# The order of rounding and eviction on ScalarE in the u products of a PEER layer

## The chip, the cores and the metric

The kernel runs on one core of a Trainium2 chip. A core has five engines that run their own instruction streams and meet only at semaphores: TensorE (PE in the profile, with its weight loads as PEld), VectorE (DVE), ScalarE (ACT), GpSimd (POOL) and SyncE (SP), which here only issues DMAs. The metric is the device time of one execution in microseconds. Before the change the median of three runs is 1938.89 us, between 1938.2 and 1939.08.

## What is computed

The reference is one residual block on 512 tokens of width 1024: a token mixer (mLSTM and differential attention), then a PEER layer. The change lies in the PEER layer, whose heart is

```
scores = einsum("thcd,hcnd->thcn", qry, sub_keys)          # 8 heads x 2 halves x 128 keys
s_top, i_top = top_k(scores, 16)                           # per half
best_s, best_pos = top_k(s_top0[:, None] + s_top1[None], 16)  # 16 of 128*128 experts
gates = softmax(best_s)
act = gelu(einsum("td,thkd->thk", h, expert_u[idx]))
out = einsum("thk,thkd->td", act * gates, expert_v[idx])
```

The kernel does this densely for 384 of the tokens' gates and 320 of their activations: it multiplies all 16384 experts in 128 tiles of 128 experts (the u products), takes Gelu of everything, multiplies by a matrix of gates that is zero almost everywhere, and multiplies by expert_v (the v products). The other tokens' experts are gathered row by row and computed on VectorE beside the products.

## The kernel before, in words

All products are float32 made of three fp32r products. An operand is cut into a rounded part (hi) and a rest (lo), and hi x hi, hi x lo and lo x hi are added.

In the stage of the u products (`experts_block`, line 2089) one step n is one tile of 128 experts:

- SP (`every`, L2176) loads raw tile n into a ring of 4 buffers, once tile n-4 has been cut (`lo_done`). Behind it SP stores the activations of tile n-4 to DRAM, after their eviction (`gelu_done`). The last 24 tiles are kept in SBUF and have no store. In some steps SP writes a piece of the gate matrix (`flush`, L2193), four pieces in four steps that follow each other, twice in each group of 16 steps.
- ScalarE rounds the raw tile: `cut` (L2351), in_uhi<-con_raw at L2356. It waits for the tile to land and for product n-2 to end, since uhi has two buffers.
- VectorE subtracts: `cut` (L2463), in_ulo<-con_raw,in_uhi at L2466.
- TensorE runs the product of tile n: 24 matmuls of 128x320 (L2274), after `lo_done` of n and the eviction of n-2 (`gelu_done`), since the sums ps_u have two buffers.
- ScalarE evicts the sums of tile n with Gelu (L2393, for the kept tiles L2395) after `u_done`.

In the first 60 steps VectorE also does the routing of the four blocks of 128 tokens (`route`, ten pieces, one a step). One piece needs an exponential on ScalarE (L2383). In the next 48 steps, the gate steps, there are one-hot matrices for the gates: VectorE makes them (L2640, L2641), ScalarE scales the rows of one (`gated_rows`, L2404, eight instructions), TensorE multiplies them after the product (16 matmuls, L2302), and ScalarE evicts the two banks (`gates`, L2415). The last 20 steps are plain. In about seven of nine gate steps, and in some of the others, VectorE works on gathered rows, and for some of these ScalarE weighs one column (L1997, L1999). Each engine runs its list in the written order. Nothing reorders it.

In ScalarE's list before the change, step n (`every`, L2367) is: the rounding of tile n+1, the small items, the wait for product n, and the eviction of tile n; then in a gate step the two evictions of gates. L2425 is a single Gelu whose result SP waits for (L2211) in one step.

Of the kernel before, what the change touches and what calls it, by code (L numbers as in the profile page):

```python
# [53 lines left out]
def wait(eng, sem, value):  # L54

    if isinstance(value, int) and value <= 0:
        return
    eng.wait_ge(sem, value)
# [1696 lines left out]
NEXP = NK  # L1755
# [333 lines left out]
def experts_block(nc, con, ring, hot, hot_all, stage, early, got, rt, A, hT, acts, gmat, x1, dst, vhi, vlo, cut_hi, cut_lo):  # L2089
# [3 lines left out]
    with Alloc(nc, "xin") as al:  # L2093
# [255 lines left out]
        @block.scalar  # L2349
        def _(act):  # L2350
            def cut(n):  # L2351

                act.wait_ge(landed[n % U_RING], 16 * (n // U_RING + 1))

                wait(act, u_done, n - 1)
                act.activation(uhi[n % 2][:], cut_of[n % U_RING], ACT.Copy).then_inc(hi_done, 1)  # L2356

            def rounded(n):
                s = n % RING
                act.wait_ge(v_in[s], 16 * (n // RING + 1))  # L2360

                wait(act, used, n - RING + 1)
                act.activation(vhi[s][:], v[s], ACT.Copy).then_inc(vhi_done, 1)  # L2363
                act.wait_ge(wt_done, n + 1)
                act.activation(whi[s][:].rearrange("p (b t) -> p b t", t=8 * G_TOK), weights(n), ACT.Copy).then_inc(whi_done, 1)

            def every(n):  # L2367
                if n < NEXP - 1:

                    cut(n + 1)  # L2370
                if n == 2:
                    act.activation(opts, con.iota[:, 0:TOPK].unsqueeze(2).to_broadcast([P, TOPK, SLOTS]),
                                   ACT.Copy).then_inc(tables, 1)
                if n > 0:
                    for r in IN_AT[n - 1]:
                        got.weigh(act, r)
                if n == NEXP - 1:
                    for h in range(2):
                        act.wait_ge(flushed[h], 64 * (N_HOT // G_STEPS))
                    rounded(0)  # L2380
                if n in EXP_AT:
                    act.wait_ge(sub_done, EXP_AT[n] + 1)
                    act.activation(ge, eg, ACT.Exp).then_inc(exp_done, 1)  # L2383
                if N_HOT0 - 1 <= n < N_TAIL0 - 1:
                    gated_rows(n + 1 - N_HOT0)
                act.wait_ge(u_done, n + 1)

                if n < STORED + RING:
                    wait(act, kept[n % 4], 16 * (n // 4))
                elif n == NEXP - in_room:  # L2390
                    act.wait_ge(flushed[0], 64 * (N_HOT // G_STEPS))
                if n < STORED:
                    act.activation(act_t[n % 4][:], ps_u[n % 2][:, 0:TU], ACT.Gelu).then_inc(gelu_done, 1)  # L2393
                else:
                    act.activation(held[n - STORED], by_block(ps_u[n % 2][:, 0:TU]), ACT.Gelu).then_inc(gelu_done, 1)  # L2395

            def gated_rows(m):

                if m == N_HOT - SIDE // G_TOK:
                    act.wait_ge(late_done, 1)  # L2400
                act.wait_ge(is_row, m + 1)
                for i in range(G_TOK):
                    at = m * G_TOK + i
                    op = act.activation(hot_i[m % 2][:, i, :], hot_i[m % 2][:, i, :], ACT.Copy, scale=slot[2][:, at:at + 1])  # L2404
                op.then_inc(gated, 1)

            def gates(gi, q):
                m = G_STEPS * gi + q
                for b in range(2):
                    act.wait_ge(g_done, 2 * m + b + 1)  # L2410
                    if q % 8 == 0 and b == 0:

                        wait(act, flushed[q // 8], 64 * gi)
                    t0 = (q % 8) * G_TOK + 4 * b
                    act.activation(stage[q // 8][:, :, t0:t0 + 4], ps_g[b].rearrange("p t i -> p i t"),  # L2415
                                   ACT.Copy).then_inc(staged, 1)

            for n in range(NEXP):
                every(n)
                if N_HOT0 <= n < N_HOT0 + N_HOT:  # L2420
                    gates((n - N_HOT0) // G_STEPS, (n - N_HOT0) % G_STEPS)
                if n == SIDE_LAST + 2:
                    last = SIDE_ENTRIES[-1]
                    act.wait_ge(got.row_free[last % ROWS], last // ROWS + 1)
                    act.activation(got.side_dots[:], got.side_dots[:], ACT.Gelu).then_inc(got.side_raw_done, 1)  # L2425
            for n in range(NEXP):
                if n > 0:
                    rounded(n)
                for r in OUT_AT[n - 1] if n else IN_AT[NEXP - 1]:
                    got.weigh(act, r)  # L2430
                if n == END:
                    act.wait_ge(got.row_free[MAIN[-1] % ROWS], MAIN[-1] // ROWS + 1)
                    act.activation(junk, got.acc[:], ACT.Square, accum_out=ss0[:]).then_inc(ss0_done, 1)
            wait(act, ss0_done, 1)
            for m in range(2 * ND):
                act.wait_ge(closed, m + 1)

                wait(act, ss_done, m)
                act.activation(junk[:, 0:512], out[m // 2][m % 2][:], ACT.Square,
                               accum_out=ss[:, m:m + 1]).then_inc(ss_done, 1)  # L2440
# [367 lines left out]
```

## Time and profile before

| | |
|---|---|
| median of 3 runs | 1938.89 us |
| profiled execution, its own time | 1935.99 us |
| its span in the profile | 1934.3 us |
| TensorE busy (PE) | 1863.7 us, 96% |
| VectorE busy | 1485.3 us, 77% |
| ScalarE busy | 819.3 us, 42% |
| stage of the u products | about 823 to 1378 us |
| stage of the v products | about 1378 to 1934 us |
| granted TensorE clock, mean | 0.992 of full speed |

The span runs from the first to the last instruction; the execution's own time is 1.7 us longer. Matmuls overlap, so a duration of 0.31 us stands beside a pitch of 0.147 us, and only the idle time of TensorE says what it lost. "Idle before, releaser" says how long an engine stood still ahead of an instruction and what ended that. An idle time of an engine that is not the bottleneck costs nothing.

### The profile page before, as it was taken

The page shows a single profiled execution, that of the slowest core. Times are in us where ns is not written, and L with a number is a line of the kernel's source. Part 1 is how long each engine was busy: PE and PEld are TensorE (multiplying, and loading weights), DVE is VectorE, ACT ScalarE, POOL GpSimd, SP SyncE. Part 2 cuts the span into 40 slices and gives each one's busy share as a digit, 9 for nine tenths or more (in the row PEclk, how much of TensorE's full clock was granted, in tenths as well). Part 3 has the DMA queues.
Part 4 walks back from the last instruction along what each step waited for, and adds up shares of the span by engine and source line. Part 5 has one row for each costly group of instructions (what it writes and reads, how often), then busy time and mean ns, then how long its engine had stood idle before and what let it go on. Part 6 is the DMA issues. An engine that isn't in the chain of part 4 may idle for free.

```text
span 1934.3 us, 28426 instructions
## 1 busy us (share of the span) xinstructions
PE 1863.7 (96%) x10366; PEld 1628.5 (84%) x10366; DVE 1485.3 (77%) x2847; ACT 819.3 (42%) x1719; POOL 550.6 (28%) x295
## 2 busy tenths in 40 slices
PE   7999999999999989999999999999999999899997
PEld 4788777888877888899999999999888778788776
DVE  4777545355466645789999999996899889899986
ACT  4110233110253253344445989884444444444443
POOL 0343201344211213201224553231244233333320
PEclk9999999999999999999999999999999999999999
DMA  7335410354211514166878899999999999999993
GB/s 284 88 109 174 152 44 23 130 199 149 75 56 44 175 52 129 66 183 225 322 273 288 304 378 362 391 391 394 346 405 414 408 412 412 390 411 412 411 391 132
DMA packets 194876, 483.68 MB, mean 250 GB/s; under 512 B 16216, under 2 KB 126992, under 8 KB 175568
## 3 DMA queue, kind: packets, MB, share of 16 engines
q1 hardware_dynamic: 166416, 314.50, 45.2%
q0 software_dynamic: 27648, 167.78, 22.0%
q8 instruction: 57, 0.93, 0.2%
q14 instruction: 51, 0.42, 0.1%
q10 hardware_dynamic: 704, 0.04, 0.0%
HBM read 435.55 MB, written 46.40 MB: 249 GB/s over the span
## 4 chain that ended last, share of the span: by engine, by line
PE 21%; DVE 20%; DMA 12%; issue 3%; ACT 1%; SPq 0%; DVEq 0%; POOLq 0%; POOL 0%; ACTq 0%
PE xin_ps_u L2274 15%; DMA experts_hot<-act_scratch 5%; DMA con_raw<-in_expert_v 4%; DVE experts_acc L2015 4%; DVE experts_rows L1988 4%; PE xin_out L2302 3%; DVE over_v_vlo L2655 3%; DMA con_raw<-in_expert_u 3%; PE xin_out L2327 2%; DVE xin_wlo L2658 2%; DVE in_ulo L2466 2%; DVE experts_rows L1977 1%; DVE xin_g L2652 1%; DVE experts_hot L2652 1%; ACT in_uhi L2356 1%
## 5 line engine op out<-in xcount | busy, mean ns | idle before, releaser
L1970 POOL DMA_INDIRECT experts_rows<-in_expert_rows,experts_idx x128 | 232.1, 1813 | 490.4 <-DVE experts_acc L2015 460.8
L2274 PE MATMUL xin_ps_u<-con_h_hi,in_uhi 128*128 128x320 f32 x1024 | 322.7, 315 | 9.7 <-DVE in_ulo L2466 6.7
L2274 PE MATMUL xin_ps_u<-con_h_lo,in_uhi 128*128 128x320 f32 x1024 | 317.1, 310 | 0.0
L2274 PE MATMUL xin_ps_u<-con_h_hi,in_ulo 128*128 128x320 f32 x1024 | 317.0, 310 | 0.0
L2327 PE MATMUL xin_out<-over_v_vhi,xin_whi 128*128 128x512 f32 x768 | 242.2, 394 | 15.3 <-DVE xin_wlo L2658 15.2
L2327 PE MATMUL xin_out<-over_v_vlo,xin_whi 128*128 128x512 f32 x768 | 239.7, 391 | 0.0
L2327 PE MATMUL xin_out<-over_v_vhi,xin_wlo 128*128 128x512 f32 x768 | 239.3, 390 | 0.0
L2274 PEld LDWEIGHTS xin_ps_u<-con_h_hi,in_uhi 128*128 128x128 f32 x1024 | 192.9, 188 | 14.4 <-DVE in_ulo L2466 11.1
L540 POOL TENSOR_TENSOR weights_wlo<-con_raw,weights_whi 128x2048 fp32r<-128x2048 f32 x29 | 133.7, 4611 | 221.7 <-DVE weights_whi L624 215.6
L2274 PEld LDWEIGHTS xin_ps_u<-con_h_lo,in_uhi 128*128 128x128 f32 x1024 | 193.1, 189 | 0.0
L2274 PEld LDWEIGHTS xin_ps_u<-con_h_hi,in_ulo 128*128 128x128 f32 x1024 | 192.8, 188 | 0.0
L2466 DVE TENSOR_TENSOR in_ulo<-con_raw,in_uhi 128x1024 fp32r<-128x1024 f32 x127 | 155.9, 1228 | 46.5 <-ACT in_uhi L2356 46.1
L2327 PEld LDWEIGHTS xin_out<-over_v_vhi,xin_whi 128*128 128x128 f32 x768 | 142.5, 189 | 54.9 <-DVE over_v_vlo L2655 19.1
L1965 POOL DMA_INDIRECT experts_rows<-in_expert_rows,experts_side_at x64 | 103.2, 1612 | 249.1 <-DVE experts_rows L1977 132.6
L2327 PEld LDWEIGHTS xin_out<-over_v_vhi,xin_wlo 128*128 128x128 f32 x768 | 144.7, 188 | 30.6
L2327 PEld LDWEIGHTS xin_out<-over_v_vlo,xin_whi 128*128 128x128 f32 x768 | 144.7, 188 | 30.5
L2363 ACT ACTIVATE over_v_vhi<-con_raw 128x1024 fp32r<-128x1024 f32 x128 | 134.6, 1051 | 75.2 <-DMA con_raw<-in_expert_v 73.3
L2015 DVE SCALAR_TENSOR_TENSOR experts_acc<-experts_rows,experts_coef,experts_acc 128x1024 f32<-128x1024 f32 x127 | 162.1, 1277 | 0.6 <-ACT experts_coef L1999 0.6
L2655 DVE TENSOR_TENSOR over_v_vlo<-con_raw,over_v_vhi 128x1024 fp32r<-128x1024 f32 x128 | 155.7, 1217 | 3.3 <-ACT over_v_vhi L2363 3.3
L1988 DVE SCALAR_TENSOR_TENSOR experts_rows<-experts_rows,con_h 128x1024 f32<-128x1024 f32 x128 | 155.7, 1216 | 0.0
L2356 ACT ACTIVATE in_uhi<-con_raw 128x1024 fp32r<-128x1024 f32 x127 | 133.6, 1052 | 9.1 <-DMA con_raw<-in_expert_u 8.8
L2404 ACT ACTIVATE experts_hot<-experts_hot,in_slot 128x128 f32<-128x128 f32 x384 | 117.3, 390 | 10.8 <-DVE experts_hot L2640 10.0
(478 smaller groups left out, 3859.3 us busy)
## 6 DMA issues: line engine op xcount, KB each, us to landing
con_raw<-in_expert_u SPq DMA_DIRECT2D x128, 512.0 KB, 7.0
con_raw<-in_expert_v SPq DMA_DIRECT2D x128, 512.0 KB, 11.3
con_raw<-in_w_in SPq DMA_DIRECT2D x36, 1024.0 KB, 6.0
act_scratch<-in_act SPq DMA_DIRECT2D x104, 160.0 KB, 4.3
experts_hot<-act_scratch SPq DMA_DIRECT2D x104, 160.0 KB, 12.4
gate_scratch<-in_stage SPq DMA_DIRECT2D x12, 1024.0 KB, 11.2
gate_scratch<-over_s_stage SPq DMA_DIRECT2D x12, 1024.0 KB, 12.4
experts_hot<-gate_scratch SPq DMA_DIRECT2D x16, 768.0 KB, 13.4
```

The source lines that it names most:

```text
L540: pool.tensor_tensor(wlo[s][:], raw[s][:], as_f32(whi[s][:]), ALU.subtract).then_inc(w_lo, 1)
L1965: pool.indirect_dma_start(out=self.rows[:, s, half * D:(half + 1) * D], out_offset=None, in_=halves, in_offset=bass.IndirectOffsetOnAxis(a ...
L1970: pool.indirect_dma_start(out=self.rows[:, s, :], out_offset=None, in_=rows, in_offset=bass.IndirectOffsetOnAxis(ap=self.idx[:, r:r + 1], ...
L1988: dve.scalar_tensor_tensor(out=u, in0=u, scalar=1.0, in1=con.h0[:], op0=ALU.mult, op1=ALU.mult, accum_out=self.coef[:, r:r + 1]).then_inc( ...
L2015: dve.scalar_tensor_tensor(out=self.acc[:], in0=v, scalar=self.coef[:, r:r + 1], in1=self.acc[:], op0=ALU.mult, op1=ALU.add).then_inc(self ...
L2274: mm = pe.matmul(ps_u[s % 2][:, 0:TU], a[s % 2][:, k, :], m[:, k, P:P + TU], start=(i == 0), stop=(i == 3 * KD - 1))
L2327: product = lambda s, t, h, w, m, **flags: pe.matmul(out[t][h][:], w[s][:, t * P:(t + 1) * P], m[s][:, h * 512:(h + 1) * 512], **flags)
L2356: act.activation(uhi[n % 2][:], cut_of[n % U_RING], ACT.Copy).then_inc(hi_done, 1)
L2363: act.activation(vhi[s][:], v[s], ACT.Copy).then_inc(vhi_done, 1)
L2404: op = act.activation(hot_i[m % 2][:, i, :], hot_i[m % 2][:, i, :], ACT.Copy, scale=slot[2][:, at:at + 1])
L2466: dve.tensor_tensor(ulo[n % 2][:], cut_of[n % U_RING], as_f32(uhi[n % 2][:]), ALU.subtract).then_inc(lo_done, 1)
L2655: dve.tensor_tensor(vlo[s][:], v[s], as_f32(vhi[s][:]), ALU.subtract).then_inc(vlo_done, 1)
```

## The change

On ScalarE the rounding of tile n+2 now stands in step n, between the wait for product n and the eviction of tile n. The rounding of tile 1 stays ahead of everything. Every tile is still rounded once, and the waits of each instruction are on the same semaphores and values.

```diff
             def every(n):
-                if n < NEXP - 1:
-
-                    cut(n + 1)
+                if n == 0:
+                    cut(1)
                 if n == 2:
                     act.activation(opts, con.iota[:, 0:TOPK].unsqueeze(2).to_broadcast([P, TOPK, SLOTS]),
                                    ACT.Copy).then_inc(tables, 1)
...
                 if N_HOT0 - 1 <= n < N_TAIL0 - 1:
                     gated_rows(n + 1 - N_HOT0)
                 act.wait_ge(u_done, n + 1)
+                if n < NEXP - 2:
+
+                    cut(n + 2)
 
                 if n < STORED + RING:
                     wait(act, kept[n % 4], 16 * (n // 4))
```

The lines below L2371 move down by two: the evictions are L2395 and L2397 after the change, the subtraction L2468, and the evictions of gates L2417.

ScalarE in a step with the exponential, of the kernel before (L2356 rounds, L2393 evicts a product, L2383 is the exponential):

```order
L2356 ACTIVATE in_uhi<-con_raw 128x1024
L2383 ACT_TABLE_LOAD
L2383 ACTIVATE over_s_stage<-over_s_stage 128x128
L2393 ACT_TABLE_LOAD
L2393 ACTIVATE in_act<-xin_ps_u 128x320
L2356 ACTIVATE in_uhi<-con_raw 128x1024
```

The same place of the changed kernel (L2395 evicts, L2382 is the exponential):

```order
L2395 ACTIVATE in_act<-xin_ps_u 128x320
L2382 ACT_TABLE_LOAD
L2382 ACTIVATE over_s_stage<-over_s_stage 128x128
L2356 ACTIVATE in_uhi<-con_raw 128x1024
L2395 ACT_TABLE_LOAD
L2395 ACTIVATE in_act<-xin_ps_u 128x320
```

The rounding that followed Gelu's table load and the eviction now stands ahead of both.

ScalarE in a gate step with a gathered row, of the kernel before (L2404 scales the one-hot rows, L2415 evicts the gate products):

```order
L2356 ACTIVATE in_uhi<-con_raw 128x1024
L1997 ACTIVATE experts_coef<-experts_coef 128x1
L1999 ACTIVATE experts_coef<-experts_coef,experts_gate 128x1
L2404 ACTIVATE experts_hot<-experts_hot,in_slot 128x128 x8
L2393 ACTIVATE in_act<-xin_ps_u 128x320
L2415 ACTIVATE in_stage<-xin_out 128x128x4 x2
```

And of the changed kernel (the same lines, L2406, L2395 and L2417 there):

```order
L1997 ACTIVATE experts_coef<-experts_coef 128x1
L1999 ACTIVATE experts_coef<-experts_coef,experts_gate 128x1
L2406 ACTIVATE experts_hot<-experts_hot,in_slot 128x128 x8
L2356 ACTIVATE in_uhi<-con_raw 128x1024
L2395 ACTIVATE in_act<-xin_ps_u 128x320
L2417 ACTIVATE in_stage<-xin_out 128x128x4 x2
```

The rounding moved ahead of three evictions, that of the product and the two of the gates. The lists of the other engines are the same.

## Rows read from the trace of the kernel before

**Rows 1.** Busy time of each engine in four stretches: us, engines, PEclk, DMA share, GB/s.

```profile
820.00:1046.00 226.00, 217.87 (x1469) 214.18 (x1467) 204.53 (x644) 101.41 (x145) 45.57 (x32) 1.00 0.74 248
1046.00:1306.00 260.00, 257.11 (x1919) 256.19 (x1920) 250.41 (x278) 232.24 (x607) 99.66 (x55) 0.99 0.98 365
1306.00:1378.00 72.00, 71.75 (x489) 71.34 (x488) 48.96 (x53) 33.00 (x63) 11.43 (x11) 1.00 0.98 366
1378.00:1934.00 556.00, 532.20 (x2302) 431.18 (x2300) 501.74 (x702) 235.85 (x468) 180.99 (x100) 0.99 0.96 382
```

**Rows 2.** Groups by line, 820 to 1378: busy us, mean ns | idle before, releasers.

```profile
L2274 PEld LDWEIGHTS xin_ps_u<-con_h_hi,in_uhi 128*128 128x128 f32 x1024 | 192.9, 188 | 14.4 <-DVE in_ulo L2466 11.1 <-issue 3.2
L2466 DVE TENSOR_TENSOR in_ulo<-con_raw,in_uhi 128x1024 fp32r<-128x1024 f32 x127 | 155.9, 1228 | 46.5 <-ACT in_uhi L2356 46.1
L2356 ACT ACTIVATE in_uhi<-con_raw 128x1024 fp32r<-128x1024 f32 x127 | 133.6, 1052 | 9.1 <-DMA con_raw<-in_expert_u 8.8 <-PEq L97 0.3
```

**Rows 3.** ScalarE in order of time: start, us, instruction, idle before and releaser.

```profile
902.77 0.44 ACT L2393 ACTIVATE in_act<-xin_ps_u 128x320 f32<-128x320 f32 x1 [2.46 <-PE xin_ps_u L2274]
...
906.29 0.44 ACT L2393 ACTIVATE in_act<-xin_ps_u 128x320 f32<-128x320 f32 x1 [2.14 <-PE xin_ps_u L2274]
...
909.32 1.28 ACT L2393 ACT_TABLE_LOAD   x1
910.61 0.44 ACT L2393 ACTIVATE in_act<-xin_ps_u 128x320 f32<-128x320 f32 x1
910.95 1.05 ACT L2356 ACTIVATE in_uhi<-con_raw 128x1024 fp32r<-128x1024 f32 x1
```

**Rows 4.** VectorE in order of time, at three places of the routing.

```profile
867.12 1.23 DVE L2466 TENSOR_TENSOR in_ulo<-con_raw,in_uhi 128x1024 fp32r<-128x1024 f32 x1 [0.73 <-ACT in_uhi L2356]
...
911.11 0.29 DVE L2527 TENSOR_TENSOR experts_gate<-over_s_stage,in_ginv 128x128 f32<-128x128 f32 x1
912.03 1.23 DVE L2466 TENSOR_TENSOR in_ulo<-con_raw,in_uhi 128x1024 fp32r<-128x1024 f32 x1 [0.62 <-ACT in_uhi L2356]
...
975.80 1.23 DVE L2466 TENSOR_TENSOR in_ulo<-con_raw,in_uhi 128x1024 fp32r<-128x1024 f32 x1 [0.20 <-ACT in_uhi L2356]
```

**Rows 5.** First weight loads of u products that had waited, three of eighteen.

```profile
918.21 0.19 PEld L2274 LDWEIGHTS xin_ps_u<-con_h_hi,in_uhi 128*128 128x128 f32 x1 [1.39 <-DVE in_ulo L2466]
...
1221.10 0.19 PEld L2274 LDWEIGHTS xin_ps_u<-con_h_hi,in_uhi 128*128 128x128 f32 x1 [1.07 <-DVE in_ulo L2466]
...
1345.45 0.19 PEld L2274 LDWEIGHTS xin_ps_u<-con_h_hi,in_uhi 128*128 128x128 f32 x1 [0.52 <-DVE in_ulo L2466]
```

**Rows 6.** SP's waits, 820 to 1380: us in total, times, longest.

```profile
SPq L2184 <- ACT in_act L2393: 298.5, 94, 6.1
...
SPq L2211 <- ACT experts_side_dots L2425: 6.8, 1, 6.8
```

**Rows 7.** Loads of u tiles: all 128 (KB, median us to landing), then one.

```profile
con_raw<-in_expert_u SPq DMA_DIRECT2D x128, 512.0 KB, 7.0
...
L2180 SPq DMA_DIRECT2D con_raw<-in_expert_u x1: 488/488/488, 914.2 to 914.2; - x1
...
DMA to landing us min/median/max: 10.7/10.7/10.7
```

**Rows 8.** ScalarE in order of time: one rounding, then two late tiles.

```profile
925.89 1.06 ACT L2356 ACTIVATE in_uhi<-con_raw 128x1024 fp32r<-128x1024 f32 x1
...
1208.30 1.06 ACT L2415 ACTIVATE over_s_stage<-xin_out 128x512 f32<-128x512 f32 x2
1211.93 1.06 ACT L2356 ACTIVATE in_uhi<-con_raw 128x1024 fp32r<-128x1024 f32 x1 [2.58 <-DMA con_raw<-in_expert_u]
...
1218.73 1.06 ACT L2356 ACTIVATE in_uhi<-con_raw 128x1024 fp32r<-128x1024 f32 x1 [1.70 <-DMA con_raw<-in_expert_u]
```

**Rows 9.** TensorE in order of time, at tile 60.

```profile
1046.26 0.39 PE L2274 MATMUL xin_ps_u<-con_h_hi,in_uhi 128*128 128x320 f32 x1 [1.87 <-issue]
...
1046.78 0.47 PE L2274 MATMUL xin_ps_u<-con_h_hi,in_uhi 128*128 128x320 f32 x1
```

## The prediction

> **What bounds the kernel now.** I read first how busy each engine is in each stretch of the stage [rows 1]. The u products run from 820 to 1378 us. TensorE is busy for 217.87 of 226 us in the first stretch (routing on VectorE), for 257.11 of 260 us in the second (the gate steps), for 71.75 of 72 us in the tail. So TensorE bounds the stage, and all its idle time there is 11.3 us. After it, in the v stage (1378 to 1934), the DMA share is 0.96 over the whole and TensorE has 24 us of idle time. The change leaves that stage alone, and what is won or lost before 1378 shifts it whole.
>
> Second, the groups by line [rows 2]. The first weight load of a u product sat idle for 14.4 us, of which 11.1 ended with in_ulo, the DVE subtraction (L2466). That subtraction waited 46.1 us for in_uhi, ScalarE's rounding (L2356), and the rounding 8.8 us for a DMA. So there is a chain: tile landed, rounding, subtraction, product. The change moves its second link.
>
> Third, the order in time on ScalarE, DVE and the weight loads [rows 3 to 5]. Plain evictions start as soon as the product ends; two of them, at 902.77 and 906.29, are 3.52 us apart: the pitch of a plain step. The rounding follows its eviction (910.61) at 910.95, so the eviction holds it back by 0.34 us. A gate step is 260/49 = 5.31 us [rows 1].
>
> Fourth, what the transfers wait for [rows 6 to 8]. SP issues the load of tile j+5 behind the store of tile j, and the store waits for the eviction of j: 298.5 us of waiting in 94 waits.
>
> **What the change does, part by part.** Nothing is added or removed: 127 roundings of 1052 ns stay [rows 2], as do the evictions. Tile n+2's rounding now starts when product n ends, and the eviction of n about 0.95 us later (a rounding takes 1.05 us, and the next instruction starts 0.1 us before its end, as 910.61 + 0.44 against 910.95 shows).
>
> 1. Plain steps, most of them: the rounding comes 0.34 us earlier, and neither TensorE nor DVE needs it: the product that wants it begins a full 3.52 us later, and the chain after the rounding is 1.05 + 1.23 us. Worth nothing. It counts only where DVE has fallen behind and goes on without a pause until TensorE waits. At 867.12 DVE waited 0.73 us for the rounding [rows 4]; all 0.34 us comes back. At 975.80 it waited 0.20 us, so 0.20 comes back. Sum: 0.54 us. If DVE had other work there it would be 0, the lower bound.
>
> 2. The steps with the exponential. ScalarE loads the exponential's table, then at 909.32 Gelu's, evicts at 910.61, and rounds at 910.95 [rows 3]. The product had ended at 906.29 + 3.52 = 909.81. In the new order the rounding starts there, ahead of the table load, 1.14 us earlier. DVE was done with its own work at 911.11 + 0.29 = 911.40 and began the subtraction at 912.03 [rows 4]. Its work began with a subtraction that itself comes 0.34 us earlier, so it is free at 911.06, and the rounding is done at 910.86. The subtraction starts at about 911.1, 0.93 us earlier. DVE then works without a pause to the product at 918.21, for which TensorE waited 1.39 us [rows 5]. So 0.93 us comes back. The pattern stands three times. From each I take 0.3 off, for loads (next step): 3 x 0.63 = 1.9 us. Bounds: 3 x 0 if DVE's own work fills in, 3 x 1.14 = 3.4.
>
> 3. The loads of this stretch. An eviction 0.95 us later lets the store and the next load start that much later, and the rounding wants its tile 0.34 us sooner. Load and rounding lose 1.3 us of margin. A load issued at 914.2 took 10.7 us [rows 7], so landed at 924.9; its tile was rounded at 925.89 [rows 8]: 1.0 us of margin, with gathered rows in flight beside it. So that rounding starts not 0.93 us earlier, but 0.6; that is the 0.3 above. The median load of the stage takes 7.0 us [rows 7], and from the eviction that releases it to the rounding that wants it there are three pitches, 10.6 us. With 3.6 us of margin it loses nothing.
>
> The evicted tile itself: product n needs the eviction of n-2. At 909.81 + 1.05 + 1.28 + 0.44 the eviction ends at 912.6, and the product that needs it starts at 913.0. It is hidden, with 0.4 us over.
>
> 4. The gate steps. Before: eviction, two evictions of the gate products (1.06 us for both [rows 8]), rounding. After: rounding, then the three. The rounding comes 0.34 + 1.06 us earlier, and more where ScalarE waited for the gate products. TensorE, busy for 257.11 of 260 us, hardly waits for it, so I count nothing. But the rounding waits for its DMA, and now the evictions stand behind that wait, where they stood ahead of it. At 1211.93 and 1218.73 ScalarE waited 2.58 and 1.70 us for tiles landing [rows 8]. TensorE's gate products need the gate evictions of the step before. Once a tile lands, 1.05 + 0.34 + 0.6 = 2.0 us go by until the first gate bank is free, and the pitch is 5.31 us. So TensorE stands still when a tile lands over 3.3 us after the product's end; before it did only at 4.8 us (5.31 us of pitch and a gate block of 5.31 - 3.52 = 1.8, less 1.05 of rounding and 1.23 of subtraction). The wait does not show in the trace of before. By these rows the tile of 1218.73 holds the gate products until 1218.73 + 2.0 = 1220.7 and the next product to about 1222.4, against 1221.10 [rows 5]: a loss of 1.3 us, the value taken. A second place like it, near 1260, where a tile landed just in time, costs 0.5 us by the same sum. Bounds: 0 (the later loads make up for it) and five bursts of gate flushes at 1.3 us each, 6.5.
>
> One more wait is in this place: SP stood 6.8 us for L2425 [rows 6], and in the new order L2425 comes 0.4 us later. That is within the 1.3.
>
> 5. The tail. Its tiles are kept in SBUF, no store stands ahead of the load, and the load waits for the subtraction alone. That is 0.34 us earlier, so loads start 0.3 us earlier and the wait of 0.52 us at 1345.45 [rows 5] shrinks by 0.3. Bounds 0 and 0.52.
>
> Sum: -0.54 - 1.9 + 1.3 + 0.5 - 0.3 = -0.9 us, to which I add nothing for the v stage. Against the profiled execution (1935.99 us, span 1934.3) this is 1935.1. The median of the runs is 1938.89, 2.9 us above that execution; on its scale the forecast is 1938.0.
>
> The rule that speaks against the change: in rows 7 and 8 one load had 1.0 us of margin and two had none. The Trainium skill's "DMA: Bandwidth & Descriptors", in its rules for kernel authors, says to issue a DMA early, compute, and wait on its semaphore late. The change does the reverse on both ends. What it would cost here is the third rival below, whose time comes from the rows.
>
> **The rivals.** What this kernel's measurement can tell from no change is about 0.2%, 3.9 us.
>
> Faster. The 2.4 us of steps 1 and 2 arrive, and step 4 costs nothing. On top, TensorE's pause of 1.87 us at 1046.26 is shortened: behind it the granted clock fell, and the matmuls took 0.47 instead of 0.31 us [rows 9]. That product took 5.29 instead of 3.51 us. If the clock stays up, 1.8 us come back. Sum: -2.4 - 0.3 - 1.8 = -4.5, so 1934.4. For it: the bound of step 2. Against: the pause is behind DVE's work without a gap, so it moves as a whole and keeps its length.
>
> Slower. The evictions behind a landing tile hold up the gate products and the next load in each of the five flush bursts, where the DMA share over the stretch is 0.98 [rows 1]. 5 x 1.3 = 6.5, and one pause of about 2 us drops the clock as at 1046, +1.8, less 2.7 won: +5.6, so 1944.5. It decides as soon as more than two tiles land 3.3 us late. For it: loads take 10 us and more there, and a late eviction starts a later load, which feeds itself. Against: between the bursts there are steps without flushes, in which the margins return, and the stretch of before lost under 3 us of TensorE in all.
>
> No effect. ScalarE's rounding was never what DVE lacked, since other work fills in: 1938.9. The waits of 0.62 and 0.73 us [rows 4] speak against it.
>
> **How the numbers follow.** The forecast 0.55, no effect 0.06, the faster rival 0.21, the slower one 0.18. The first two lie within 0.2%, so same 0.61, faster 0.21, slower 0.18. The forecast's own range, from the bounds of steps 1 to 5 that are near their rows, is 1935.5 to 1941. The range for 8 in 10 reaches to both rivals: 1933.5 to 1944.5.
>
> **What would show it.** Right: the wait at about 918 falls from 1.39 to under 0.7 us, likewise its two fellows; DVE's wait for in_uhi falls from 46.1 to near 30 us (0.34 us in each of 48 waits); the product of tile 60 starts about 2.4 us earlier than 1046.26; ScalarE's wait for landing tiles rises from 8.8 us; gate products (L2302) show a new wait for the evictions (L2417 after) near 1220. Wrong: TensorE's idle time from 820 to 1046 unchanged (step 2); no wait of L2302 on ScalarE (step 4); TensorE losing over 6 us from 1046 to 1306 (the slower rival); a start of the v stage that moved while the end did not, or the other way round.

## The result, and the profile after

The kernel became slower: median 1947.91 us against 1939.08 us of the kernel before, 15 runs each. The ratio is 1.0036, its 95% interval 1.0025 to 1.0048, so 4.8 to 9.3 us. The forecast was 1938.0 with a range up to 1944.5. One execution of 4785.03 us, among the six of the kernel with the early rounding in the gate steps alone (below), lies far outside all others and is left out of its ratio and median.

The profiled execution after is one of 1951.13 us, span 1949.4: 15.1 us longer than that of before, where the medians differ by 8.8. Busy time of each engine in four stretches, columns as in [rows 1]:

```profile
820.00:1046.00 226.00, 220.17 (x1488) 216.77 (x1486) 205.07 (x653) 101.04 (x139) 45.57 (x31) 1.00 0.72 245
1046.00:1306.00 260.00, 251.90 (x1867) 250.54 (x1866) 247.34 (x274) 225.01 (x597) 94.20 (x55) 0.99 0.96 353
1306.00:1378.00 72.00, 68.48 (x464) 68.25 (x463) 45.72 (x49) 33.24 (x69) 9.17 (x9) 0.98 0.97 372
1378.00:1934.00 556.00, 538.28 (x2353) 437.95 (x2352) 505.83 (x700) 239.60 (x472) 176.49 (x100) 0.99 0.97 385
```

Against [rows 1] TensorE has 2.3 us less idle time in the first stretch (1.0 when counted from the start of the stage, below) and 5.2 us more in the second (8.1 against 2.9), while the DMA share there fell from 0.98 to 0.96. The stretches no longer hold the same steps, so I went by the first and last instruction of each kind. The gate products of before, then of after (ns of one, then first and last start):

```profile
L2302 PE MATMUL xin_out<-experts_hot x768: 270/275/275, 1051.4 to 1306.2; 128*128 128x128 f32 x192
```

```profile
L2302 PE MATMUL xin_out<-experts_hot x768: 270/275/422, 1053.3 to 1317.9; 128*128 128x128 f32 x192
```

The gate stretch is 254.8 us before and 264.6 after. The same reading for all stages, in us (a few of the experiments below are in the table too; one profile each):

| kernel | u start | u start to tile 60 | gate stretch | v start | span |
|---|---|---|---|---|---|
| before | 823.1 | 223.1 | 254.8 | 1377.2 | 1934.3 |
| after | 826.0 | 222.2 | 264.6 | 1389.1 | 1949.4 |
| early in routing only | 823.1 | 221.5 | 255.2 | 1374.2 | 1934.3 |
| early in gate steps only | 824.6 | 223.2 | 261.8 | 1385.9 | 1945.6 |
| after, late store | 824.0 | 219.7 | 257.6 | 1376.9 | 1935.8 |
| gate steps, late store | 823.3 | 223.4 | 255.4 | 1377.8 | 1933.7 |

Of the 15.1 us, 2.9 lie ahead of the stage, where nothing changed, 9.0 in the u products (554.1 against 563.1), and 3.2 behind them; this is how much single executions differ outside the change. The 9.0 are +9.8 in the gate stretch and about -1 in the routing.

What waits for what, by lines (820 to 1395; columns as in [rows 2]):

```profile
L2274 PEld LDWEIGHTS xin_ps_u<-con_h_hi,in_uhi 128*128 128x128 f32 x1024 | 193.7, 189 | 11.1 <-DVE in_ulo L2468 7.3 <-issue 3.7
L2468 DVE TENSOR_TENSOR in_ulo<-con_raw,in_uhi 128x1024 fp32r<-128x1024 f32 x127 | 156.0, 1229 | 51.3 <-ACT in_uhi L2356 51.0
```

And as a list of waits over the same stretch (engine, who waited, for whom: us in total, times, longest):

```profile
ACT in_uhi L2356 <- DMA con_raw<-in_expert_u: 15.0, 7, 4.3
PEld xin_out L2302 <- issue: 9.3, 5, 3.8
PE xin_out L2302 <- ACT over_s_stage L2417: 5.3, 2, 3.5
PE xin_out L2302 <- ACT in_stage L2417: 2.7, 1, 2.7
```

```profile
SPq L2184 <- ACT in_act L2395: 295.7, 93, 8.7
```

The u product's wait for the subtraction fell from 11.1 to 7.3 us [rows 2]: the chain that the change shortens did get shorter. In its place the gate products (L2302) wait for ScalarE's eviction, and ScalarE for landing tiles, 15.0 us against 8.8. SP's longest wait for an eviction rose from 6.1 [rows 6] to 8.7.

The list has only part of ScalarE's waits for tiles: where ScalarE also waited for a product, it can put a wait for a landing down to PE or to "issue". I therefore matched each of the 48 tiles rounded in the gate stretch with the landing of its own load, in one profile of each kernel. "Late" is a rounding that starts within 0.1 us of the landing. The last column is how long after the end of a product its eviction starts.

| kernel | late tiles | ScalarE idle ahead of them, us | landing to rounding, median us | product's end to its eviction, median us |
|---|---|---|---|---|
| before | 5 | 7.8 | 5.9 | 0.9 |
| after | 14 | 23.8 | 3.6 | 2.0 |
| gate steps, late store | 6 | 10.4 | 6.1 | 1.7 |
| after, late store | 3 | 8.5 | 6.6 | 1.5 |

So the margin of a typical tile shrank by 2.3 us, and the tiles that had almost none before came late.

The first of these places, on the weight loads, ScalarE and SP of the kernel after (start, us, instruction, idle before):

```profile
1178.41 2.65 PEld L2302 LDWEIGHTS xin_out<-experts_hot 128*128 128x128 f32 x16 [2.96 <-issue]
1213.83 1.86 PEld L2302 LDWEIGHTS xin_out<-experts_hot 128*128 128x128 f32 x16 [2.02 <-issue]
1315.18 2.87 PEld L2302 LDWEIGHTS xin_out<-experts_hot 128*128 128x128 f32 x16 [3.75 <-issue]
```

```profile
1176.43 1.06 ACT L2356 ACTIVATE in_uhi<-con_raw 128x1024 fp32r<-128x1024 f32 x1 [4.88 <-PE xin_ps_u L2274]
1177.39 0.42 ACT L2395 ACTIVATE in_act<-xin_ps_u 128x320 f32<-128x320 f32 x1
1177.71 1.08 ACT L2417 ACTIVATE in_stage<-xin_out 128x512 f32<-128x512 f32 x2
```

```profile
1160.31 3.62 SPq L2180 DMA_DIRECT2D con_raw<-in_expert_u  x1
...
1166.85 0.45 SPq L2180 DMA_DIRECT2D con_raw<-in_expert_u  x1
...
1168.64 0.48 SPq L2180 DMA_DIRECT2D con_raw<-in_expert_u  x1
1177.84 0.32 SPq L2184 DMA_DIRECT2D act_scratch<-in_act  x1
1178.20 0.43 SPq L2180 DMA_DIRECT2D con_raw<-in_expert_u  x1
```

The load issued at 1160.31 took 16.0 us to landing:

```profile
L2180 SPq DMA_DIRECT2D con_raw<-in_expert_u x1: 3621/3621/3621, 1160.3 to 1160.3; - x1
...
DMA to landing us min/median/max: 16.0/16.0/16.0
```

Read these together. The tile landed at 1160.3 + 16.0 = 1176.3 and ScalarE rounded it at 1176.43, after 4.88 us of standing still. The row names PE as the releaser, but the product that this rounding waits for had long ended; it was the DMA, whose landing time fits to 0.1 us. Behind the rounding came the product's eviction (1177.39) and the gates' (1177.71), and with the first gate bank free the gate products went on at 1178.41. The product's eviction also let SP issue its store at 1177.84 and, behind it in SP's list, the next load at 1178.20, 9.6 us after the last one. The same stretch of the kernel before has loads every 3.3 to 5.7 us there:

```profile
1161.56 0.49 SPq L2180 DMA_DIRECT2D con_raw<-in_expert_u  x1
1164.51 0.32 SPq L2184 DMA_DIRECT2D act_scratch<-in_act  x1
1164.88 0.50 SPq L2180 DMA_DIRECT2D con_raw<-in_expert_u  x1
1170.21 0.32 SPq L2184 DMA_DIRECT2D act_scratch<-in_act  x1
1170.58 0.44 SPq L2180 DMA_DIRECT2D con_raw<-in_expert_u  x1
```

So a late tile delays the next load. That is a loop: landing, rounding, eviction, store, load, landing. From 1045 to 1320 us four pairs of neighbouring loads lie over 8 us apart (9.6, 12.5, 8.7 and 8.5); in the kernel before it is one (14.9). After a pause of TensorE the sixteen weight loads of the gates took 2.65 and 2.87 us instead of 1.86: the granted clock had fallen for a while. From here to 1232, then to 1318, and below them the same windows of the kernel before:

```profile
1172.00:1232.00 60.00, 53.91 (x390) 53.25 (x390) 51.61 (x57) 48.67 (x132) 13.68 (x8) 0.97 0.91 340
1232.00:1318.00 86.00, 82.46 (x617) 81.99 (x615) 78.09 (x80) 74.50 (x201) 18.88 (x12) 0.99 0.99 370
```

```profile
1172.00:1232.00 60.00, 57.55 (x434) 57.17 (x433) 55.76 (x60) 52.49 (x144) 15.89 (x8) 1.00 0.96 363
1232.00:1318.00 86.00, 85.96 (x640) 85.77 (x640) 79.52 (x82) 74.45 (x197) 24.81 (x14) 1.00 1.02 383
```

Here are 9.6 us of TensorE's idle time, where the kernel before has 2.5, and 0.03 x 60 + 0.01 x 86 = 2.7 us by the clock. In the first of the two the DMA share is 0.91 against 0.96: the DMA engines had room while tiles were late. This fits loads that were issued late. It does not show that as the only reason, since the landing of 16.0 us was itself long (the load of the same tile took 13.0 before).

### The profile page after: what moved, and what is told of

It reads as the page before. It is cut to its first block, busy times and chain, and to the rows that moved or that the text cites. A ratio compares the mean times of both kernels' runs of the same rounds, so it can differ in the third digit from the quotient of the medians.

```text
span 1949.4 us, 28321 instructions
## 1 busy us (share of the span) xinstructions
PE 1870.0 (96%) x10366; PEld 1633.4 (84%) x10366; DVE 1488.2 (76%) x2847; ACT 816.7 (42%) x1719; POOL 539.3 (28%) x295
## 4 chain that ended last, share of the span: by engine, by line
PE 21%; DVE 17%; DMA 14%; issue 2%; ACT 1%; SPq 1%; DVEq 0%; POOLq 0%; POOL 0%; ACTq 0%
PE xin_ps_u L2274 16%; DMA experts_hot<-act_scratch 7%; DMA con_raw<-in_expert_v 4%; DVE experts_rows L1988 3%; DVE experts_acc L2015 3%; PE xin_out L2302 3%; DVE over_v_vlo L2657 3%; DMA con_raw<-in_expert_u 3%; PE xin_out L2327 2%; DVE xin_wlo L2660 2%; DVE in_ulo L2468 1%; DVE experts_rows L1977 1%; DVE xin_g L2654 1%; DVE experts_hot L2654 1%; ACT in_uhi L2356 1%
## 5 line engine op out<-in xcount | busy, mean ns | idle before, releaser
L1970 POOL DMA_INDIRECT experts_rows<-in_expert_rows,experts_idx x128 | 219.3, 1714 | 516.6 <-DVE experts_acc L2015 482.6
L2356 ACT ACTIVATE in_uhi<-con_raw 128x1024 fp32r<-128x1024 f32 x127 | 134.2, 1057 | 180.5 <-PE xin_ps_u L2274 146.5
L2274 PEld LDWEIGHTS xin_ps_u<-con_h_hi,in_uhi 128*128 128x128 f32 x1024 | 193.7, 189 | 11.1 <-DVE in_ulo L2468 7.3
L540 POOL TENSOR_TENSOR weights_wlo<-con_raw,weights_whi 128x2048 fp32r<-128x2048 f32 x29 | 133.7, 4610 | 223.2 <-DVE weights_whi L624 217.1
L2468 DVE TENSOR_TENSOR in_ulo<-con_raw,in_uhi 128x1024 fp32r<-128x1024 f32 x127 | 156.0, 1229 | 51.3 <-ACT in_uhi L2356 51.0
L2406 ACT ACTIVATE experts_hot<-experts_hot,in_slot 128x128 f32<-128x128 f32 x384 | 117.5, 392 | 16.7 <-DVE experts_hot L2642 16.4
```

The costliest lines, as they stand in the source:

```text
L540: pool.tensor_tensor(wlo[s][:], raw[s][:], as_f32(whi[s][:]), ALU.subtract).then_inc(w_lo, 1)
L1970: pool.indirect_dma_start(out=self.rows[:, s, :], out_offset=None, in_=rows, in_offset=bass.IndirectOffsetOnAxis(ap=self.idx[:, r:r + 1], ...
L2274: mm = pe.matmul(ps_u[s % 2][:, 0:TU], a[s % 2][:, k, :], m[:, k, P:P + TU], start=(i == 0), stop=(i == 3 * KD - 1))
L2468: dve.tensor_tensor(ulo[n % 2][:], cut_of[n % U_RING], as_f32(uhi[n % 2][:]), ALU.subtract).then_inc(lo_done, 1)
```

## Experiments

Two theories stood at the start. **Feedback**, the loop: the product's eviction stands later, so SP's store, and the load behind it, come later, tiles land late, and that feeds itself. **Bank wait**: the gates' evictions stand behind a landing tile, and TensorE's gate products wait for them; loads are not at fault. Both fit the trace after. All ratios are against the kernel before on the same chip, over 10 to 12 runs (5 for the first), with 95% intervals.

**Which part of the stage costs.** The early rounding in one group of tiles, the old place in all others. The condition is the only difference among four kernels:

```diff
-                if n < NEXP - 1:
+                if n < NEXP - 1 and not early(n + 1):
...
+                if n < NEXP - 2 and early(n + 2):
+                    cut(n + 2)
```

Gate steps, `early = lambda k: N_HOT0 + 2 <= k < N_TAIL0 + 2`:

> Only in the 48 gate steps does the rounding stand ahead of the evictions; the routing steps and the tail are as before. Theory G (gate evictions queue behind a landing tile and TensorE's gate products wait for them): the whole loss of the change is here, TensorE's L2302 waits 5 to 9 us for the gate evictions, and the time is 8 to 12 us above before, as the routing's gain is missing. Rival R (the later product eviction delays the next load everywhere, routing included): a part only, under 5 us. Rival V (the loss comes in the v stage): about 0, and no wait of L2302 on ScalarE.

Measured: 1.0048 (1.0035 to 1.0062), median 1949.55 against 1939.41. The whole loss lies here. Gate products waited for ScalarE again:

```profile
PE xin_out L2302 <- ACT over_s_stage L2419: 4.7, 3, 2.4
PE xin_out L2302 <- ACT in_stage L2419: 1.8, 1, 1.8
```

Routing steps, `early = lambda k: 2 <= k < N_HOT0 + 2`:

> Only in the first 60 steps does the rounding stand ahead of the eviction. Theory G: 1 us faster than before (0 to 2.4), the gate stretch as before. Rival R: slower than before by 2 to 4 us, TensorE's idle time from 820 to 1046 grown and tiles landing later. Rival V: no difference.

Measured: 0.9981 (0.9967 to 0.9995), median 1935.78: faster, by 1.0 to 6.4 us. No gate product waited for ScalarE.

Tail, `early = lambda k: N_TAIL0 + 2 <= k`:

> Only in the last 18 steps, whose tiles have no store, does the rounding stand ahead of the eviction. Theory G: within 0.5 us of before, in either direction, since there are no gate products here. Rival V (what is new at the transition to the v products costs time later): slower by over 3 us.

Measured: 1.0000 (0.9988 to 1.0012). Nothing that can be seen.

The steps with the exponential alone, `early = lambda k: k - 2 in EXP_AT`:

> Only in the four steps with the exponential does the rounding stand ahead of Gelu's table load and the eviction. If the gain of the routing comes from these steps and the losses there from loads that start later in all the others: 1.5 to 3 us faster than before, and the three waits of 1.3 to 1.4 us of TensorE shrink to 0.4 to 0.7 with no new waits between them. If the gain needs the other steps too: 0 to 1 us faster.

Measured: 0.9997 (0.9986 to 1.0008). Inconclusive on a gain of 1.9 us. In its profile tile 60 starts 1.3 us earlier after the stage's start than before.

**Which eviction must not be late.** In the gate steps only, the rounding is put between the product's eviction and those of the gates:

```diff
                 else:
                     act.activation(held[n - STORED], by_block(ps_u[n % 2][:, 0:TU]), ACT.Gelu).then_inc(gelu_done, 1)
+                if n < NEXP - 2 and early(n + 2):
+                    cut(n + 2)
```

> Only the gate steps are changed: eviction of the product, then the rounding, then the two evictions of gates. The load behind the store is released as before; the gate evictions stand behind the landing. Theory G (the gate evictions behind the landing are the cost): 7 to 10 us slower than before, like the run with all three behind the rounding, and L2302 waits over 4 us for ScalarE. Rival L (the product's eviction behind the landing delays store and next load, and late tiles make the rest): within 2 us of before.

Measured: 1.0020 (1.0008 to 1.0032), 1.6 to 6.2 us slower. The product's eviction stands where it stood before, so SP's activation stores are not delayed by the order, though the flushes, which need the gates' evictions, are. Neither expectation was met: it is less than the 7 to 10 us of the bank wait alone and, at its median of 3.3 us, more than the 2 us of the feedback. What is left is the wait for the bank: one pause of 4.7 us and one of 1.5.

```profile
PE xin_out L2302 <- ACT over_s_stage L2419: 4.7, 1, 4.7
PE xin_out L2302 <- ACT in_stage L2419: 1.5, 1, 1.5
```

Then the other way round: gates' evictions, rounding, product's eviction.

```diff
                 act.wait_ge(u_done, n + 1)
+                if N_HOT0 <= n < N_HOT0 + N_HOT:
+                    gates((n - N_HOT0) // G_STEPS, (n - N_HOT0) % G_STEPS)
+                if n < NEXP - 2 and early(n + 2):
+                    cut(n + 2)
...
                 every(n)
-                if N_HOT0 <= n < N_HOT0 + N_HOT:
-                    gates((n - N_HOT0) // G_STEPS, (n - N_HOT0) % G_STEPS)
```

> Only the gate steps are changed: the two evictions of gates first, then the rounding, then the product's eviction, so that store and next load come later and the gate banks are free as early as they can be. Theory G: no wait of L2302 on ScalarE and 0 to 3 us slower than before. Rival L: 5 to 10 us slower, with tiles landing later and TensorE waiting for the subtraction.

Measured: 1.0049 (1.0033 to 1.0065), as slow as the changed order, though no gate product waited for an eviction any more. TensorE waited for the subtraction and, once, for the gathered gates:

```profile
PE xin_ps_u L2274 <- DVE in_ulo L2470: 8.7, 12, 1.8
...
PE xin_out L2292 <- DVE experts_side_gate L2628: 5.0, 1, 5.0
```

The 5.0 us are lateness of a tile as well: VectorE stood still for 3.92 us for the rounding of a tile that had just landed, and its work on the gathered gates stands behind that subtraction.

So the loss can be had in full without any wait for a gate bank, and with the product's eviction in its old place more than half of it goes. But this order also puts the product's eviction further back than the changed one does: it starts 3.3 us after the product's end in the median, against 2.0 there and 0.9 before. The equal times therefore do not show that the bank wait costs nothing in the changed order.

**Loosening the loop.** SP stores tile j one load later, so that load j+5 no longer stands behind the eviction of j. Load j+6 does, so the coupling is not cut but given one more step of room. In the next four kernels:

```diff
-                    if n - 4 < STORED:
-                        sp.wait_ge(gelu_done, n - 3)
-                        sp.dma_start(acts[(n - 4) * P:(n - 3) * P, :], act_t[n % 4][:]).then_inc(kept[n % 4], 16)
+                    if 0 <= n - 5 < STORED:
+                        sp.wait_ge(gelu_done, n - 4)
+                        sp.dma_start(acts[(n - 5) * P:(n - 4) * P, :], act_t[(n - 5) % 4][:]).then_inc(kept[(n - 5) % 4], 16)
```

The changed kernel with it:

> The changed kernel, and SP stores the activations of tile j behind the load of tile j+5, not ahead of it, so that a load is released by the subtraction alone. Rival L: the loss is gone, 0 to 4 us faster than before. Theory G with the load's release as the feedback that makes tiles late: 3 to 6 us of the loss of 8 gone. Theory G alone: as slow as the changed kernel, 5 to 9 us above before.

Measured: 0.9994 (0.9977 to 1.0011) where it was 1.0036. SP's waits:

```profile
SPq L2180 <- DVE in_ulo L2470: 231.7, 108, 5.9
SPq L2184 <- ACT in_act L2397: 144.9, 89, 4.0
```

The load now waits mostly for the subtraction, its own condition, and the longest wait for an eviction fell from 8.7 to 4.0. One wait of a gate product, of 4.2 us, is left in this profile. The kernel before with the same edit, to see whether it is worth something by itself:

> The kernel before with the same move of the store. Here the load starts up to 2.6 us earlier in plain steps. ScalarE's wait of 8.8 us for landing tiles and the waits of TensorE behind it (about 1.1 and 0.5 us) shrink: 0 to 2 us faster. If the DMA engines are simply full in the gate steps: no difference.

Measured: 0.9999 (0.9986 to 1.0012). It is not.

The gate steps alone, the whole loss, with the late store:

> In the gate steps all three evictions stand behind the rounding, and SP's store stands behind the next load. Two links are now proposed: B, the gate banks (about 3.5 us, as measured with the product's eviction left ahead), and S, the store and next load behind a late product eviction (the rest of 9.4 us). With both: S is cut, so 2 to 4 us slower than before, L2302 still waits for ScalarE. If S is the whole: 0. If the late store only helped by the routing: 7 to 9 us slower.

Measured: 1.0000 (0.9986 to 1.0015) where it was 1.0048. The waits of gate products of over half a microsecond fell from four to one, and nothing but the store's place differs:

```profile
1207.83 1.86 PEld L2302 LDWEIGHTS xin_out<-experts_hot 128*128 128x128 f32 x16 [2.41 <-issue]
```

The order with the product's eviction last, with the late store:

> Gate evictions, rounding, product eviction, and the store behind the next load. Neither B nor S is left: within 2 us of before, where the same order with the old store was 9.5 us slower. If the wait for landing itself on ScalarE's list costs (VectorE's one-hot rows scaled later), still 5 us or more.

Measured: 1.0006 (0.9989 to 1.0023) where it was 1.0049. Its single profile (span 1944.6) still has a gate stretch of 259.4 us. One late tile is left in it, rounded at 1210.05 after ScalarE had stood still for 5.95 us, and behind it TensorE waits 6.3 us for the gathered gates (1.6 before), which is about the whole 4.6 us by which the stretch is longer.

**A late eviction without a landing ahead of it.** Rounding in its old place, but in the gate steps the gates' evictions ahead of the product's:

```diff
+            early = lambda k: False
...
                 act.wait_ge(u_done, n + 1)
+                if N_HOT0 <= n < N_HOT0 + N_HOT:
+                    gates((n - N_HOT0) // G_STEPS, (n - N_HOT0) % G_STEPS)
```

The old call of the gates' evictions goes, as above.

> The rounding stays last in the gate steps, as before; only the product's eviction moves behind the two gate evictions, by about 1.5 us in every one of them, with no landing ahead of it. If a load that starts 1.5 us later in each gate step costs by itself: 4 us or more slower. If it is the landing of one tile ahead of the eviction that feeds itself: within 2 us of before.

Measured: 1.0033 (1.0018 to 1.0049), 3.5 to 9.5 us slower. The expectation of the feedback theory, which wanted a landing ahead of the eviction, failed. ScalarE there:

```profile
1096.56 0.60 ACT L2421 ACTIVATE over_s_stage<-xin_out 128x512 f32<-128x512 f32 x1
1097.39 0.60 ACT L2421 ACTIVATE over_s_stage<-xin_out 128x512 f32<-128x512 f32 x1 [0.24 <-PE xin_out L2302]
1097.89 0.43 ACT L2399 ACTIVATE in_act<-xin_ps_u 128x320 f32<-128x320 f32 x1
```

The evictions of the gates wait for the gate products, and the product's eviction now waits with them. Over the 48 steps it starts 2.3 us after the end of its product in the median, 1.5 us later than before (0.9), and that alone makes tiles late: ScalarE waited 19.9 us for landing tiles, where it was 8.8 before, and TensorE stood still for 2.7 us in one piece at 1209 and for 3.0 us at 1218 for the gathered gates. The changed order shifts the eviction by 1.2 us in the median (2.0), so the plain shift here is at least as large as there, and it costs 0.33% where the changed gate steps cost 0.48%, with intervals that overlap. What the landing adds was not told apart from this plain shift.

**The version that wins.** Early rounding in the routing steps, with the late store:

> The likely best version: the rounding early in the 60 routing steps alone, and the store behind the next load. Loads start up to 1.3 us earlier there than with the old store, so the 3.6 us won by the routing order alone should grow by 0 to 1.5: 3.5 to 5 us faster than before. If the late store harms the gate steps by what it saves: 2 to 3.5 us.

Measured: 0.9974 (0.9960 to 0.9988), median 1934.92: faster than both kernels. From the stage's start to tile 60 it takes 219.7 us (before 223.1), without the late store 221.5. Its interval overlaps that of the early routing without the late store (0.9967 to 0.9995) and that of the changed kernel with it (0.9977 to 1.0011), so neither the worth of the late store here nor a rest of the cost in the gate steps is told apart from nothing.

## Why the prediction was wrong

**The step that failed is step 4**, the gate steps, with the value of 1.8 us taken for them, and within it a sentence of step 3 on which it rested: "With 3.6 us of margin it loses nothing." The gate steps alone cost 6.8 to 12.0 us (ratio 1.0048). The sum counted only the gate bank at two landings that the trace of before showed late, and left the release of the next load at nothing. But step 3 worked out the margin for a plain step: with a loss of 1.3 us, a pitch of 3.52 us and the median landing of the whole stage, 7.0 us. In a gate step, by the prediction's own terms, the release comes 0.95 us later and the rounding 0.34 + 1.06 = 1.40 us earlier, a loss of 2.35 us; the table above has 2.3. The profile of before, with its window narrowed to the gate stretch (1046 to 1306), shows this:

```profile
con_raw<-in_expert_u SPq DMA_DIRECT2D x49, 512.0 KB, 10.2
```

```profile
DMA to landing us min/median/max: 3.7/10.2/16.9
```

Three pitches of a gate step are 15.9 us. Against the median that leaves 5.7 us, and against the longest landing nothing. The tiles that landed late [rows 8] were the sign. In place of two late tiles with a loss of 1.8 us the runs show 14 late tiles, three pauses of TensorE for gate banks of 1.8 to 3.5 us, and a loss that goes to 1.0000 when the load no longer stands behind the late eviction. The prediction's own sign for this, TensorE losing over 6 us from 1046 to 1306, came with 8.1 us.

**The slower rival had the mechanism**, "a late eviction starts a later load, which feeds itself". It got 0.18, at 5.6 us net where 8.8 was measured. Its five bursts became three pauses of 2 to 4 us (by the weight loads) and a clock that fell behind two of them, not one. Its price per place, 1.3 us, came from a landing taken as fixed, whereas landings moved too. What spoke against it, that margins return between bursts, was not enough: over 8 us passed between loads in four places where it had been one, and TensorE lost 9.6 us from 1172 to 1318, against 2.5 before. That a late eviction costs is shown by the runs; that the lateness feeds itself is seen in the trace and was not tested apart from the shift. The forecast's sign "gate products show a new wait near 1220" came too, at 1178, 1213 and 1315.

**Step 2**, the exponential steps. The wait of 1.39 us at 918 [rows 5] was to fall below 0.7:

```profile
919.84 0.19 PEld L2274 LDWEIGHTS xin_ps_u<-con_h_hi,in_uhi 128*128 128x128 f32 x1 [0.69 <-DVE in_ulo L2468]
927.58 0.19 PEld L2274 LDWEIGHTS xin_ps_u<-con_h_hi,in_uhi 128*128 128x128 f32 x1 [0.70 <-DVE in_ulo L2468]
931.76 0.19 PEld L2274 LDWEIGHTS xin_ps_u<-con_h_hi,in_uhi 128*128 128x128 f32 x1 [0.66 <-DVE in_ulo L2468]
936.18 0.19 PEld L2274 LDWEIGHTS xin_ps_u<-con_h_hi,in_uhi 128*128 128x128 f32 x1 [0.90 <-DVE in_ulo L2468]
```

It did, to 0.69, and its fellows fell from 1.34 to 0.64 and 0.79, the last just missing the sign. The fourth step with the exponential, which the prediction left out, kept its wait (1.35 us before at 881.03, 1.33 after). But two new waits follow at once, one of 0.59 before has grown to 0.90 (936.18), and ScalarE waited for tiles there:

```profile
925.21 1.06 ACT L2356 ACTIVATE in_uhi<-con_raw 128x1024 fp32r<-128x1024 f32 x1 [4.29 <-DMA con_raw<-in_expert_u]
929.39 1.06 ACT L2356 ACTIVATE in_uhi<-con_raw 128x1024 fp32r<-128x1024 f32 x1 [2.80 <-DMA con_raw<-in_expert_u]
```

Tile 60 came 1.0 us earlier, not 2.4. The 0.3 us per place taken off for loads (step 3) was too little here. With the late store the changed kernel gains 3.4 us up to tile 60 (219.7 against 223.1), near the 2.4 + 0.9 that the sum had without that deduction. So in these single profiles steps 1 and 2 are right in mechanism and about right in size, and in the changed kernel the loads took most of it back. The medians for the routing alone differ by -3.6 us; -2.4 is inside the interval (-1.0 to -6.4).

**VectorE's wait** for the rounding was to fall from 46.1 to about 30 us. It rose to 51.0. With the late store it is 42.2, so nine of the difference go with the late tiles. Why the rest of the fall did not come I have not traced.

**Step 5**, the tail: nothing measurable, and 0.3 could not be measured.

**The faster rival** wanted a shorter pause at tile 60. The pause stayed 1.87 us, as the argument against it said, and the clock fell behind it again.

The rule weighed in the prediction, in the Trainium skill's "DMA: Bandwidth & Descriptors" (rules for kernel authors): issue a DMA early, compute, and wait for its semaphore late. The runs agree where margins were short: loads whose release came 1.5 us later in the gate steps cost 0.33%, and loads moved ahead of the store that had held them gave back 0.42 to 0.48%. In the kernel before, the same move gave nothing (0.9999).

What stays open: how much of the loss is the plain shift of the eviction by 1.2 us and how much the wait behind a landing; how much of it passes through the gate banks (with the product's eviction in its old place it was 1.6 to 6.2 us); and whether the bank wait costs anything once the loop has one more step of room (the interval of that kernel leaves -2.7 to +2.9 us).

## What to carry to other kernels

Before you put an instruction that waits for a transfer ahead of another on an in-order engine, follow what the second one releases, down to the next transfer: here an eviction released a store, and the store stood ahead of the next load in SP's list. Work out the margin of a load with the landing times of the very stretch, in its longest cases, not with a median over the stage. Where a load stands behind a store that waits for something else, move the store one place back; it gave nothing to the kernel before, and it was worth about 8 us to one whose evictions came later.

## What the runs showed of the hardware

- Issuing a load took 0.43 us in the median over the stage, but 3.62 us at 1160.31, next to flushes of the gate matrix. In the gate stretch of the kernel before 9 of 49 issues took over 3 us, up to 5.86. The landing of the load of 1160.31 took 16.0 us, against 3.7 at the least in that stretch before. SP is held in such an issue too.
- The same pause of 1.87 us at tile 60 was followed by a fall of the granted clock to 1.2 GHz in some executions and not in others. Before, the first gate product comes 5.1 us after that tile's start; with the early rounding in the routing only, 3.6 us:

```profile
1044.56 0.38 PE L2274 MATMUL xin_ps_u<-con_h_hi,in_uhi 128*128 128x320 f32 x1 [1.87 <-issue]
```

The clock row of that kernel shows full speed behind it, that of the kernel after shows half speed a little later:

```profile
1046.00:1048.00 2.00, 2.00 (x15) 2.00 (x14) 2.00 (x4) 0.08 (x1) 1.70 (x2) 1.00 1.02 420
```

```profile
1050.00:1052.00 2.00, 2.00 (x9) 2.00 (x9) 2.00 (x4) 0.47 (x2) 1.70 (x2) 0.50 1.04 426
```

So a difference of 1.5 us at such a place between two single profiles need not come from the edit. The mean clock of one and the same kernel, the one before, lies between 0.988 and 0.994 of full speed in its 29 executions beside the first experiments.
